# Memory keys and values as split products, with value projections between the score units

## What is computed

```python
h = rms_norm_2(x, mem_norm_pre[l])
m = rms_norm_2(mem, mem_norm_kv[l])
q = (h @ wq).reshape(B, S, MEM_HEADS, MEM_HEAD_DIM)
k = (mem_n @ wk).reshape(B, M, MEM_HEADS, MEM_HEAD_DIM)
v = (mem_n @ wv).reshape(B, M, MEM_HEADS, MEM_HEAD_DIM)
s = jnp.einsum('bshd,bmhd->bhsm', q, k).astype(F32) * (MEM_HEAD_DIM ** -0.5)
p = jax.nn.softmax(s, axis=-1).astype(v.dtype)
return jnp.einsum('bhsm,bmhd->bshd', p, v).reshape(B, S, D) @ wo
```

## Time and profile before

| | |
|---|---|
| times of three runs | 1893.26, 1887.43, 1893.10 us |
| median | 1893.1 us |
| span of the profiled execution, first to last instruction | 1891.5 us |
| TensorE busy, share of the span | 1849.7 us, 98% |
| VectorE, ScalarE, POOL busy | 1067.8, 711.2, 150.0 us |
| mean granted TensorE clock | 0.985 |
| memory stage, first key to first output product | 1318.8 to 1461.3 us |

### The profile page before, as it was taken

One profiled execution on the slowest core, in us unless ns is written; L12 is line 12 of the kernel. 1 busy time (PEld: TensorE's weight loads), 2 busy tenths in 40 slices (PEclk: granted clock), 3 DMA queues, 4 the chain that ended last, 5 costly groups with the idle time before them and its releaser, 6 DMA issues.

```text
span 1891.5 us, 26769 instructions
## 1 busy us (share of the span) xinstructions
PE 1849.7 (98%) x10668; PEld 1468.5 (78%) x10668; DVE 1067.8 (56%) x1782; ACT 711.2 (38%) x1293; POOL 150.0 (8%) x65
## 2 busy tenths in 40 slices
PE   8999999999999999999999999999999999999998
PEld 5778788887887888888888776348885778888887
DVE  5558656586645644445443665652615398777434
ACT  5543544535445321221234624653404442222333
POOL 0033323323002000000000000000000000000000
PEclk9999999999899999999999999999999999999999
DMA  5412122121134323223222351004422212322321
GB/s 185 80 35 79 46 68 68 36 90 35 46 134 132 102 89 104 96 89 107 93 90 90 87 121 36 1 6 129 134 90 67 90 60 96 111 89 91 109 73 62
DMA packets 178833, 157.94 MB, mean 83 GB/s; under 512 B 32625, under 2 KB 175534, under 8 KB 178698
## 3 DMA queue, kind: packets, MB, share of 16 engines
q1 hardware_dynamic: 168320, 152.61, 26.1%
q0 software_dynamic: 1248, 3.19, 1.2%
q10 hardware_dynamic: 9163, 0.72, 0.3%
HBM read 152.77 MB, written 3.73 MB: 83 GB/s over the span
## 4 chain that ended last, share of the span: by engine, by line
PE 88%; DVE 7%; ACT 3%; issue 1%; DMA 1%; SPq 0%; ACTq 0%; DVEq 0%
PE bank L708 13%; PE bank L710 13%; PE bank L709 13%; PE bank L809 5%; PE bank L810 5%; PE bank L811 5%; PE bank L880 4%; PE bank L698 4%; PE bank L882 4%; PE bank L881 4%; PE bank L1279 2%; PE bank L987 1%; PE bank L1262 1%; PE bank L998 1%; PE bank L1009 1%
## 5 line engine op out<-in xcount | busy, mean ns | idle before, releaser
L1427 ACT ACTIVATE w_hi<-ring 128x2048 fp32r<-128x2048 f32 x122 | 233.4, 1914 | 547.6 <-PE bank L710 392.7
L708 PE MATMUL bank<-h_hi,w_hi 128*128 128x512 f32 x1056 | 413.0, 391 | 2.2 <-DVE w_lo L2000 2.0
L710 PE MATMUL bank<-h_hi,w_lo 128*128 128x512 f32 x1056 | 411.0, 389 | 0.0
L709 PE MATMUL bank<-h_lo,w_hi 128*128 128x512 f32 x1056 | 410.9, 389 | 0.0
L2000 DVE TENSOR_TENSOR w_lo<-ring,w_hi 128x2048 fp32r<-128x2048 f32 x99 | 226.6, 2289 | 258.9 <-ACT w_hi L1427 258.9
L708 PEld LDWEIGHTS bank<-h_hi,w_hi 128*128 128x128 f32 x1056 | 198.2, 188 | 46.9 <-issue 4.4
L710 PEld LDWEIGHTS bank<-h_hi,w_lo 128*128 128x128 f32 x1056 | 198.2, 188 | 41.4
L709 PEld LDWEIGHTS bank<-h_lo,w_hi 128*128 128x128 f32 x1056 | 198.3, 188 | 41.3 <-issue 0.5
L2710 POOL TENSOR_TENSOR w_lo<-ring,w_hi 128x2048 fp32r<-128x2048 f32 x23 | 105.5, 4589 | 1241.0 <-ACT w_hi L1427 1146.2
L809 PE MATMUL bank<-h_hi,w_hi 128*128 128x512 f32 x432 | 170.3, 394 | 1.7 <-DVE arena L2670 1.0
L811 PE MATMUL bank<-h_hi,w_lo 128*128 128x512 f32 x432 | 168.7, 391 | 0.0
(11 more groups left out here) (417 smaller groups left out, 2539.2 us busy)
## 6 DMA issues: line engine op xcount, KB each, us to landing
ring<-in_sc_w_in SPq DMA_DIRECT2D x32, 1024.0 KB, 5.4
ring<-in_gdn_w_in SPq DMA_DIRECT2D x24, 1024.0 KB, 5.4
ring<-in_w_up SPq DMA_DIRECT2D x22, 1024.0 KB, 5.0
ring<-in_gdn_w_out SPq DMA_DIRECT2D x8, 1024.0 KB, 5.0
ring<-in_sc_w_out SPq DMA_DIRECT2D x8, 1024.0 KB, 4.9
ring<-in_w_down SPq DMA_DIRECT2D x8, 1024.0 KB, 5.1
ring<-in_w_in SPq DMA_DIRECT2D x4, 1024.0 KB, 5.7
ring<-in_w_mk SPq DMA_DIRECT2D x4, 1024.0 KB, 5.2
```

The source lines that it names most:

```text
L708: pe.matmul(o, a_hi(k), b_hi(k), start=(k == tiles[0]), stop=False)
L709: pe.matmul(o, a_hi(k), b_lo(k), start=False, stop=False)
L710: mm = pe.matmul(o, a_lo(k), b_hi(k), start=False, stop=(k == tiles[-1]))
L1427: act.activation(w_hi[:, plan[n]["pair"], :], ring[:, n % 2, :], ACT.Copy).then_inc(w_hi_ready, 1)
```

## The change

The raw slabs of keys and values become split ones. The memory rows are kept as `mem_hi` and `mem_lo` in `mem_parts`, in the place of `mem_out`, which nothing used; ScalarE writes the one, VectorE the other from the same bank. `q0_slab` goes; all 16 slabs of the stage pass through `ring`. GpSimd subtracts key slabs 0, 2 and 3, VectorE all others. Two value chunks (head 0) stay ahead of the scores, and the other six come inside score units 2, 4, 7, 9, 12 and 15, between a unit's scores and the turning of the unit two before it. In `plan` the last two value slabs also count head-product chunks (4 and 6 and 2 more). TensorE has 24 fp32r matmuls of 256 columns for a key or value chunk, where it had 8 fp32 ones.

```diff
+        with nc.sbuf_tensor("mem_parts", [P, 2 * KD * MEM], mybir.dt.float32r) as mem_parts:
+            mem_hi, mem_lo = [mem_parts[:, n * KD * MEM:(n + 1) * KD * MEM].rearrange("p (k m) -> p k m", k=KD) for n in range(2)]
...
         MEM0 = len(plan)
-        slab_of("raw", 2, n=4)
+        slab_of("split", 2, n=10)
+        slab_of("split", 4)
+        slab_of("split", 6)
+        V3_END = plan[-1]["end"]
         plan[-1]["end"] += 2
-        plan[-1]["splits"] += 1
-        Q0 = {"used": plan[-1]["end"], "splits": plan[-1]["splits"], "pair": (plan[-1]["splits"] + 1) % 2}
-        slab_of("split", 2, n=3)
-        slab_of("raw", 2, n=4)
-        plan[-1]["end"] += KD
         MOUT = len(plan)
+        MV0 = plan[MEM0 + 7]["end"]
+        value_at = {2: (1, 0), 4: (1, 1), 7: (2, 0), 9: (2, 1), 12: (3, 0), 15: (3, 1)}
+        value_chunk = [MV0 + n for n in (0, 1, 2, 3, 6, 7, 10, 13)]
+        head_chunk = [MV0 + n for n in (4, 5, 8, 9, 11, 12, 14, 15)]
...
-        by_vector |= set(range(ends[MEM0 + 3] - 2, ends[MEM0 + 6])) | set(range(ends[FF1 - 1], ends[FF1 + FK - 1]))
-        by_vector |= set(range(ends[MOUT - 1] - KD, ends[MOUT - 1]))
+        by_vector |= set(range(ends[MEM0 + 3], ends[MEM0 + 7])) | set(range(ends[FF1 - 1], ends[FF1 + FK - 1]))
+        by_vector |= set(head_chunk)
...
-            load(w_mk_2[0].rearrange("(k p) c -> p k c", p=P)[:, :, 0:256], wide(256))
-            sp.wait_ge(mem_turned, KD)
-            sp.dma_start(q0_slab.rearrange("p (k c) -> p k c", k=KD), w_mq_2[0].rearrange("(k p) c -> p k c", p=P)[:, :, 0:256])\
-                .then_inc(q0_in, 16)
             for w in (w_mk_2, w_mq_2, w_mv_2, w_mo_2):
                 for n in range(4):
-                    if w in (w_mk_2, w_mq_2) and n == 0:
-                        continue
                     load(w[0].rearrange("(k p) c -> p k c", p=P)[:, :, 256 * n:256 * n + 256], wide(256))
...
-                    chunk(slab(pos, 128 * side), KD, lambda k: mem_T[:, k, :], MEM)
+                    b, c = take_bank(None), P * side
+                    product3(psum[b][:, 0:MEM], lambda k: w_hi[:, pos, k * 256 + c:k * 256 + c + P],
+                             lambda k: w_lo[:, pos, k * 256 + c:k * 256 + c + P],
+                             lambda k: mem_hi[:, k, :], lambda k: mem_lo[:, k, :]).then_inc(chunk_done, 1)
                     if n + side == 0:
                         out_sum()
-            pe.wait_ge(h_ready, 32)
-            pe.wait_ge(split_ready, Q0["splits"])
-            chunk3(Q0["pair"], 0)
+            q_slab = next_slab()
+            chunk3(q_slab, 0, tile_wait=lambda k: pe.wait_ge(h_ready, 24 + k + 1))
             norm_sum()
-            chunk3(Q0["pair"], P)
+            chunk3(q_slab, P)
             for n in range(3):
                 pair3()
-            for n in range(4):
-                pos = next_slab()
-                for t in range(MT):
-                    chunk(lambda k: mem_T[:, k, t * P:(t + 1) * P], KD, lambda k: ring[:, pos, k * 256:k * 256 + 256], 256)
-            all_out()
+
+            def mem_values(t):
+                if t == 0:
+                    st["slab"] = next_slab()
+                b, tok_t = take_bank(None), slice(t * P, (t + 1) * P)
+                product3(psum[b][:, 0:256], lambda k: mem_hi[:, k, tok_t], lambda k: mem_lo[:, k, tok_t],
+                         *wide3(st["slab"])).then_inc(chunk_done, 1)
+
+            mem_values(0)
+            mem_values(1)
+            all_out(2)
...
+                if n in value_at:
+                    mem_values(value_at[n][1])
...
+                    pe.wait_ge(*taken(value_chunk[2 * h + 1]))
...
-                        act.activation(mem_T[:, j, :], psum[4 + j % 2][:, 0:MEM], ACT.Copy, scale=KVW(j)).then_inc(mem_turned_out, 1)
+                        act.activation(mem_hi[:, j, :], psum[4 + j % 2][:, 0:MEM], ACT.Copy, scale=KVW(j)).then_inc(mem_hi_ready, 1)
...
-            post_norm(2, beside=mem_beside, ahead=lambda pair: split_hi(XOUT + 2 + pair) if pair < 2 else None)
+            post_norm(2, beside=mem_beside, last=lambda: split_hi(MEM0 + 1),
+                      ahead=lambda pair: split_hi(XOUT + 2 + pair) if pair < 2 else split_hi(MEM0) if pair == 3 else None)
...
-                if k == 4:
-                    act.wait_ge(q0_in, 16)
-                    act.activation(w_hi[:, Q0["pair"], :], q0_slab, ACT.Copy).then_inc(w_hi_ready, 1)
+                if k in (1, 4):
+                    split_hi(MEM0 + 2 + k // 4)
...
-            split_hi(MEM0 + 4)
+                if c == 6:
+                    split_hi(MEM0 + 4)
             norm_rms()
-            st["chunk"] += 2 * KD
-            split_hi(MEM0 + 5, used=Q0["used"], arrived=plan[MEM0 + 5]["arrived"])
-            split_hi(MEM0 + 6, used=plan[MEM0 + 4]["end"], arrived=plan[MEM0 + 6]["arrived"])
-            for n in range(4):
-                for t in range(MT):
-                    act.wait_ge(chunk_done, st["chunk"] + 1)
-                    act.activation(mem_v[:, t, 256 * n:256 * n + 256], psum[st["chunk"] % 4][:, 0:256], ACT.Copy).then_inc(act_out, 1)
-                    st["chunk"] += 1
-            pv0 = st["chunk"]
+            for n in range(MEM0 + 5, MEM0 + 10):
+                split_hi(n)
+
+            def mem_values_out(n):
+                c = value_chunk[n]
+                act.wait_ge(chunk_done, c + 1)
+                act.activation(mem_v[:, n % 2, n // 2 * 256:n // 2 * 256 + 256], psum[c % 4][:, 0:256], ACT.Copy).then_inc(act_out, 1)
+
+            mem_values_out(0)
+            mem_values_out(1)
+            st["chunk"] += 4 * KD
...
+                if n in value_at:
+                    mem_values_out(2 * value_at[n][0] + value_at[n][1])
...
-                if n in (5, 9):
-                    split_hi(MOUT + (n - 5) // 4)
+                    for k in (m // 2 - 1, m // 2):
+                        act.wait_ge(chunk_done, head_chunk[k] + 1)
+                        act.activation(h_hi[:, k, :], psum[head_chunk[k] % 4][:, :], ACT.Copy).then_inc(out_hi, 1)
+                if n in (1, 6, 11):
+                    split_hi(MEM0 + 10 + n // 5)
+                if n == 17:
+                    split_hi(MOUT + 1, used=V3_END, arrived=plan[MOUT + 1]["arrived"])
...
-            def split_q0(k):
-                if k == 5:
-                    dve.wait_ge(w_hi_ready, Q0["splits"])
-                    dve.tensor_tensor(w_lo[:, Q0["pair"], :], q0_slab, w_hi[:, Q0["pair"], :].bitcast(F32), ALU.subtract)\
-                        .then_inc(split_ready, 1)
-
-            post_norm(beside=mem_scale, between=split_q0, ahead=lambda pair: split_lo(XOUT + 2 + pair) if pair < 2 else None)
+                if 3 <= k < 7:
+                    for j in (2 * k - 6, 2 * k - 5):
+                        dve.wait_ge(mem_hi_ready, j + 1)
+                        dve.scalar_tensor_tensor(out=mem_lo[:, j, :], in0=psum[4 + j % 2][:, 0:MEM], scalar=KVW(j),
+                                                 in1=mem_hi[:, j, :].bitcast(F32), op0=ALU.mult, op1=ALU.subtract).then_inc(mem_turned_out, 1)
+
+            post_norm(beside=mem_scale, last=lambda: split_lo(MEM0 + 1), ahead=lambda pair: split_lo(XOUT + 2 + pair) if pair < 2 else None)
             split_lo(MEM0 + 4)
             norm_ready()
-            q0 = plan[MEM0 + 3]["end"] - 2
+            split_lo(MEM0 + 5)
+            q0 = plan[MEM0 + 3]["end"]
             for c in range(KD):
                 of_bank(q0 + c, mem_q[:, c, :]).then_inc(dve_out, 1)
-                if c in (1, 3):
-                    split_lo(MEM0 + 5 + c // 2)
+                if c % 2:
+                    split_lo(MEM0 + 6 + c // 2)
...
-                if n in (6, 10):
-                    split_lo(MOUT + (n - 6) // 4)
+                        out_low(k, psum[head_chunk[k] % 4][:, :], done=dve_out)
+                if n in (2, 7, 12, 18):
+                    split_lo(MEM0 + 10 + n // 5)
...
-            split_lo(FF1)
+            for n in (MEM0, MEM0 + 2, MEM0 + 3, FF1):
+                split_lo(n)
```

More of the change, by code:

```diff
@@ L1445, in square_tile, with post_norm @@
                 act.activation(sq[:, k % 2, :], src, ACT.Square).then_inc(square_ready, 1)
[L1447 removed]
+            def post_norm(layer, early=None, y_T=y_T, beside=lambda k: None, ahead=lambda pair: None, wide=False, last=lambda: None):
                 for k in range(KD):
@@ L2024, in next_tiles, with post_norm @@
                     out_low(k, source[:, KD * a + k, :])
-            def post_norm(y_T=y_T, parts=True, beside=lambda k: None, between=lambda k: None, ahead=lambda pair: None, second=None, summed=0):
+            def post_norm(y_T=y_T, parts=True, beside=lambda k: None, between=lambda k: None, ahead=lambda pair: None, second=None, summed=0, last=lambda: None):
                 layer = st["layer"]
```

22 lines of the change are left out of this document (7 added, 15 removed).

## The result

The changed kernel takes 1895.4 us (median of 20 runs, 1888.4 to 1900.8), the kernel before, beside it on the same chip, 1891.5 (20 runs, 1887.4 to 1898.4). The ratio is **1.0025, with a 95% interval of 1.0015 to 1.0035**: 2.8 to 6.6 us slower, with +4.7 by the ratio itself and +3.9 between the two medians. The forecast was +4.9 us.

A forecast was written before the change was run, and what follows sets the result against it. The prediction took TensorE, working 98% of the span, to bound the kernel. Its terms +11.1 + 1.7 + 0.5 - 8.4 = +4.9 us on 1893.1 gave 1898.0 us, range 1889 to 1902.

The forecast's parts named there:

- The account that had a chance of 0.50: Main forecast for the memory stage: POOL delays VectorE's norm chain, values and scores gain; +4.9 us, range 1895 to 1901.
- norm chain and query slab: Before the queries: POOL's subtractions hold up VectorE and the query slab follows the sums; queries start 11.1 us later.
- half clock at the queries' start: Start of the queries: TensorE's clock falls after the pause, +1.7 us, with 0 and 3.4 as ends.
- second query slab: Queries: ScalarE copies slab MEM0+5 only after the inverse norm, so TensorE waits; +0.5 us, ends 0 and 1.
- values and scores: Last stretch of the memory stage: cheaper value chunks, six between score units, shorten 68.7 us to 60.3; -8.4 us.
- Keys cheaper, but hidden: Key products: eight split chunks save 4.6 us, but only the first counts, starting the norm chain 0.57 us earlier.
- Norm chain: VectorE ahead of the queries: two POOL subtractions of 4.6 us make the addition of tile 6 5.8 us late.
- The waits of TensorE: Ahead of the queries: TensorE waits about 4.3 us for MEM0+2, 5.4 for MEM0+3 and 5.9 for the query slab.
- The walk through the units: Values and scores, engine orders followed unit by unit: 54.5 us plus waits of 0.7, 0.6, 2.5 and 2.0, giving 60.3.
- Rival 1: Norm chain: VectorE isn't held up by POOL, queries start 3.1 us late; -4.8 us, 1888.3; chance 0.12.
- rival 2: Norm chain: POOL loses the race, the chain keeps pace but keys come late; +2.5 us, 1895.6; chance 0.15.
- rival 3: Waits add up: longer half clock, last head product at half clock, two more ScalarE waits; +9.1 us, 1902.2; chance 0.23.

The follow-up runs named there:

- e2: The changed kernel with VectorE's low part of the first query slab ahead of the seven sums of squares and ScalarE's copy one key chunk earlier; 1.0008 of before.
- e1: The changed kernel with key slabs MEM0+2 and MEM0+3 subtracted by VectorE between norm-chain tiles instead of by POOL; 0.9997 of before.
- e8: The changed kernel with unused TensorE products in its three pauses; one profiled execution, no ratio, queries' stretch 45.03 us.
- e4: The changed kernel with all eight value chunks ahead of the score units and output slabs split where before had them; 1.0022 of before.
- a1: The changed kernel run once more, nothing altered, for a second trace; span 1896.9 us.

## Why the prediction was right, and where it was not

**Outcome.** +4.9 us forecast, +3.9 between the medians, +2.8 to +6.6 by the interval, +3.3 to +4.3 by the traces. The account that had a chance of 0.50 is what happened; it was right in where the loss lies and what causes it. That the total came so near is in part luck: the gain of the values was put 1.6 us too small and the loss at the mixer's turned rows at nothing, and the two errors run against each other. The terms came out so:

| term | predicted | measured |
|---|---|---|
| norm chain and query slab, from the first key product | +11.1 | 39.93 - 29.15 = +10.8 |
| half clock at the queries' start | +1.7 | +1.4 and +2.3 |
| second query slab | +0.5 | +0.37 |
| values and scores | -8.4 | -9.97 |
| mixer's projection with the turned memory rows | 0 | +0.70 |

**Keys cheaper, but hidden.** Right. A split chunk took 2.83 us to the next mark, and the start of the chain gained 0.6; no more of the keys is on the path. e2 shows it: its last key product started at 1357.12, and TensorE then waited 1.70 us for the query slab.

**Norm chain.** Right, step by step: POOL's two subtractions of 4.51 and 4.54 us, VectorE's operations of 4.49 and 4.53, each ending some 0.55 us after POOL's, as in the row that the prediction used. From the chain's first scaling to the addition of tile 6 is 1352.45 - 1329.74 = 22.71 us, before 1342.10 - 1325.53 = 16.57: 6.1 longer, where 5.8 + 0.57 = 6.4 had been said. (The prediction called the chain's operations alike in that both inputs lie in SBUF; the two that were held are of another kind than the addition of its row, and behaved the same.) The last part, the sums and the slab behind them, is right as well. e1 shows that it is POOL's company: VectorE doing the same subtractions itself was 3.0 us faster. The Trainium skill, "SBUF — State Buffer", section "SBUF: two separate sides", has an exclusive lock that the first to start keeps for its whole instruction. The rows agree: each of the three POOL subtractions held one VectorE operation until some 0.55 us after its end. That the port and not the memory behind it is what is locked, no run here shows.

**The waits of TensorE.** 4.3, 5.4 and 5.9 us were predicted; 4.23, 2.95 and 4.05 came. The sum counted key products at full speed; those after a pause ran in part at half clock and filled part of the next pause (the clock of the whole key stretch is 0.87). That cost nothing on the path, as the keys are in slack there.

**The clock.** The size was a choice between 0 and 3.4, taken in the middle; it is 1.4 in one trace and 2.3 in the other. The experiments say what it hangs on here: the last pause ahead of the queries. e2 has the change's first two pauses (4.23 and 2.96 us) and a last one of 1.70, and its queries ran at full clock; e8 filled the pauses and theirs did too.

**Values and scores: this term was mis-sized**, by 1.6 us, -8.4 said and -9.97 measured. The walk through the units was the step that failed: it gave 60.3 us for the stretch, which took 58.35. The waits came out at 0.44 at the start (0.7 said), none before the first head product (0.6 said), 1.65 at unit 12 (2.5 at unit 14 said) and 0.41 + 1.03 before the last head (2.0 said). The stretch before was taken as 68.7 us where it is 68.32, an error of 0.4 the other way. That no half clock would come in it was right, but not the reason, that TensorE is full up to the last head: it waited 0.41 and 1.03 us there, and e4 kept the full clock with all the waits of before. e4 adds that I had the reasons in the wrong proportion: of the 10.0 us the cheaper chunks and the clock at the last head gave 7.5, the placing only 2.45, and that in the spacing of the units and not in the waits that the walk went by. The pace of the value products is near that of the row used (0.120): 22.61 us in e4 for eight chunks of 24 are 0.118 each. The 109 ns from the Trainium skill ("TensorE: Matmul & The Clock Gate", section "Back-to-back issue gap", which gives the formula for a single product) would have made them 20.9 us, by estimate. The runs don't bear it out, though it would have put the forecast of this term nearer by accident.

**The mixer's turned rows** were costed at nothing. Each pair of banks is now read by ScalarE and then by VectorE, and TensorE waits 0.42 us for the second reader; with the steps around it the projection takes 0.70 us longer.

**Rival 1** (VectorE isn't held up) and **rival 2** (POOL loses the race) fall by the rows of 4.49 and 4.53 us. Of **rival 3** only its first part came in a1, where the half clock lasted longer; the last head stayed at full clock and the wait at the end of the units was smaller, not larger.

## What to carry to other kernels

A change of two halves should be costed, and run, as two halves: here one won 10 us and the other lost 13, and the sum looked like nothing. An engine without work is not free if it holds up one that stands on the path: a POOL subtraction of 4.5 us cost VectorE 3.7, where its own would have taken 2.3. When several microseconds come and go by chance ahead of the place of interest, compare stretches between marks that both kernels have; those that waits set repeated to 0.1 us where the whole span did not to 10, and only a stretch with a half clock in it differed by more (46.43 and 47.37).
